# Differential attention on one core: both score maps of a step in one piece, the nine transposes in one piece behind them

## The chip, the cores and the metric

One core of a Trainium2 chip runs the whole program. The metric is the device time of one execution in microseconds (us); lower is better.

## The reference, cut to what matters

The program is one inference step of a two-layer backbone over 1024 latent and 128 context tokens: an even layer (long convolution and retention), an odd layer (differential attention), and after each a routed mixture of 16 experts. The change lies in the attention of the odd layer. Of each of 8 heads there are two maps of scores with 64 columns each; the second map's softmax, times lambda, is taken from the first's:

```python
def diff_attention(q, k, v, lam):
    B, Lq, H, _, d = q.shape
    nb = Lq // Q_BLOCK
    qb = q.reshape(B, nb, Q_BLOCK, H, 2, d).transpose(1, 0, 2, 3, 4, 5)
    scale = d ** -0.5

    def block(qi):
        s = jnp.einsum("bqhmd,bkhmd->bhmqk", qi, k).astype(jnp.float32) * scale
        p = jax.nn.softmax(s, axis=-1)
        a = p[:, :, 0] - lam * p[:, :, 1]
        return jnp.einsum("bhqk,bkhe->bqhe", a.astype(v.dtype), v)

    o = lax.map(block, qb)
    return o.transpose(1, 0, 2, 3, 4).reshape(B, Lq, H, 2 * d)
```

A block of 128 latent queries reads 1152 keys (1024 latent, 128 cached context); a block of context queries reads the 128 context keys alone. After the heads come a norm over each head's 128 columns and the output projection.

## The kernel before

All work is written out by hand, engine by engine, as straight lines of instructions with semaphores; nothing is rescheduled. The list `steps` has 72 steps (h, q): 8 heads, and for each 8 blocks of latent queries (q = 0 to 7) and one of context queries (q = 8). An iteration n of TensorE's loop (the function `attention`, from L1260) belongs to step n but computes the scores of step n + 2, so that softmax has time.

- `scores(n, m)` (L1219 to L1239) writes map m of step n into three of TensorE's result banks, 0 to 2 for m = 0 and 3 to 5 for m = 1. The contraction has 64 rows, so two multiplications stand beside each other in the two halves of the 128 rows: L1229 in one half, L1231 in the other (for this each head's queries and keys are also kept with halves swapped, in the ring buffer), then L1233 for the cached keys. The maps change halves. A context step has L1237 alone. Before it writes, it waits on `a.e` until ScalarE has read the same banks for step n - 1.
- On VectorE `maxima(n)` (L2108) takes the negated row maxima of both maps; on ScalarE `exps(n)` (L1560) turns both maps into exponentials in `eb` with their row sums; on VectorE `mix(n)` (L2116 to L2120) subtracts the scaled second map from the first.
- `turn` (L1241 to L1253) transposes the nine 128x128 pieces of the mixed map with TensorE. Eight (L1248) go to banks 6 and 7, four each; the ninth (L1253) goes to bank 6 again, so it waits on `a.tev` until ScalarE's first copy out of bank 6 is done. A context step has one piece.
- ScalarE's `evacuate` (L1568) copies bank 6, bank 7 and the ninth piece into `aT`.
- The product with the values (L1279, nine pieces added up in bank 7) waits on `a.tev` for the copies of bank 6 and bank 7; its ninth piece waits for the ninth copy. VectorE's L2135 reads the result and signals `a.oev`; L2137 sums its squares.
- At q = 2 of each head but the first, behind the product, the previous head's normed output is turned by the same nine transposes (called the head turn below) and copied by ScalarE to `yT`.

ScalarE's order in iteration n is `evacuate` of step n, then `exps(n + 2)`, then at q = 2 the copies of the head turn. VectorE's is `mix(n + 1)`, `maxima(n + 2)`, then L2135 of step n.

In the loop of TensorE the second map stands between the eight transposes and the ninth:

```python
                    if n + 2 < len(steps):
                        scores(n + 2, 0)
                    pe.wait_ge(*at("a.a", n + 1))
                    if n:
                        pe.wait_ge(*at("a.oev", n))
                    probs = lambda t: eb[:, n % 2, 0, t * P:(t + 1) * P]
                    turn(probs, done, nt, ninth=False)
                    if n + 2 < len(steps):
                        scores(n + 2, 1)
                    turn(probs, done, nt, first=False)
```

Of the kernel before, what the change touches and what calls it, by code (L numbers as in the profile page):

```python
# [109 lines left out]
def build(nc, a, out, tab):  # L110

    with ExitStack() as ctx:
# [32 lines left out]
        def common(name):  # L145
            head, _, tail = name.partition(".")
            pre, k = shared.get(head + ".", (head + ".", 0))
            name = pre + tail if _ else name
            base, off = carried.get(name, (name, 0))
            return base, off + (k * adds[base] if k else 0), name  # L150

        def s(name):

            name = common(name)[0]
            if name not in made:
                made[name] = ctx.enter_context(nc.semaphore(name))
            return made[name]
# [4 lines left out]
        def at(name, value):  # L162

            base, off, name = common(name)
            return s(base), value + off + ahead.get(name, 0)
# [230 lines left out]
        steps = [(h, q) for h in range(AH) for q in range(T)]  # L396
# [345 lines left out]
        def _(pe):  # L742
# [463 lines left out]
            def attention():  # L1206

                for h in range(AH):
                    i = tr(ps[:, 6 + h // 4, (h % 4) * P:(h % 4 + 1) * P], kTa[:, h, LAT:NT], ident[:, :])
                i.then_inc(s("a.kt"), 1)  # L1210
                pe.wait_ge(*at("a.ck", 16))
                for h in range(AH):
                    i = tr(ps[:, 4 + h // 4, (h % 4) * P:(h % 4 + 1) * P], ckrow[:, h * P:(h + 1) * P], ident[:, :])
                i.then_inc(s("a.kt"), 1)
                pe.wait_ge(*at("a.kctx", 2))
                pe.wait_ge(*at("a.ckT", 2))
                pe.wait_ge(*at("q.rope", 16))

                def scores(n, m):  # L1219

                    h, q = steps[n]
                    if n:
                        pe.wait_ge(*at("a.e", 2 * (n - 1) + m + 1))
                    if q < 8:
                        pe.wait_ge(*at(f"a.sw{h % 2}", 64 * (h // 2 + 1)))
                        near, far = slice(64 * m, 64 * m + 64), slice(64 - 64 * m, 128 - 64 * m)
                        own, other = qTa[near, h, q * P:(q + 1) * P], qTs[h % 2][far, q * P:(q + 1) * P]
                        for c in (0, 256):
                            mm(ps[:, 3 * m, c:c + 256], own, kTa[near, h, c:c + 256],  # L1229
                               start=True, stop=True, tile_position=(64 * m, 0))  # L1230
                            mm(ps[:, 3 * m + 1, c:c + 256], other, kTs[h % 2][far, c:c + 256],  # L1231
                               start=True, stop=True, tile_position=(64 - 64 * m, 0))
                        i = mm(ps[:, 3 * m + 2, 0:P], own, ckT[near, h, :],  # L1233
                               start=True, stop=True, tile_position=(64 * m, 0))
                    else:
                        near = slice(64 * m, 64 * m + 64)
                        i = mm(ps[:, 3 * m, 0:P], qTa[near, h, LAT:NT], kTa[near, h, LAT:NT],  # L1237
                               start=True, stop=True, tile_position=(64 * m, 0))
                    i.then_inc(s("a.s"), 1)  # L1239

                def turn(src, before, nt, first=True, ninth=True, oev=None):  # L1241

                    if first:
                        pe.wait_ge(*at("a.tev", before))
                        for t in range(min(nt, 8)):
                            if t == 4 and oev:
                                pe.wait_ge(*at("a.oev", oev))
                            i = tr(ps[:, 6 + t // 4, (t % 4) * P:(t % 4 + 1) * P], src(t), ident[:, :])  # L1248
                            if t % 4 == 3 or t == nt - 1:
                                i.then_inc(s("a.t"), 1)  # L1250
                    if ninth and nt == 9:
                        pe.wait_ge(*at("a.tev", before + 1))
                        tr(ps[:, 6, 0:P], src(8), ident[:, :]).then_inc(s("a.t"), 1)  # L1253

                for n in range(2):
                    for m in range(2):
                        scores(n, m)
                done = 0
                for n, (h, q) in enumerate(steps):
                    nt = 9 if q < 8 else 1  # L1260
                    if n + 2 < len(steps):
                        scores(n + 2, 0)
                    pe.wait_ge(*at("a.a", n + 1))
                    if n:
                        pe.wait_ge(*at("a.oev", n))
                    probs = lambda t: eb[:, n % 2, 0, t * P:(t + 1) * P]
                    turn(probs, done, nt, ninth=False)
                    if n + 2 < len(steps):
                        scores(n + 2, 1)
                    turn(probs, done, nt, first=False)  # L1270
                    done = tev_of[n]
                    pe.wait_ge(*at("a.tev", done - (nt == 9)))
                    if n == 0:
                        pe.wait_ge(*at("a.cv", 16))
                    for t in range(nt):
                        if t == 8:
                            pe.wait_ge(*at("a.tev", done))
                        v = cv[:, h * P:(h + 1) * P] if t == 8 else va[:, t if q < 8 else 8, h * P:(h + 1) * P]
                        i = mm(ps[:, 7, 0:P], aT[:, t * P:(t + 1) * P], v, start=t == 0, stop=t == nt - 1)  # L1279
                    i.then_inc(s("a.pv"), 1)  # L1280
                    if q == head_step and h:
                        pe.wait_ge(*at("a.on", h))
                        turn(lambda t: ohs[(h - 1) % 2][:, t, :], done, 9, oev=n + 1)
                        done = head_tev[h - 1]
                pe.wait_ge(*at("a.on", AH))
                pe.wait_ge(*at("a.oev", len(steps)))
                turn(lambda t: ohs[(AH - 1) % 2][:, t, :], done, 9)
                pe.wait_ge(*at("a.tev", head_tev[-1]))
                pe.sem_inc(s(f"slot{swap_unit % NS}_free"), 1)
# [11 lines left out]
            norm("n11.")  # L1301
            project("q.", odd_jobs)
            attention()
            out_project(1, outo_units)
            norm("n21.")
# [886 lines left out]
```

## Time and profile before

| | |
|---|---|
| time, median of 3 runs | 3970.93 us (3963.55 to 3975.09) |
| the profiled execution's own time | 3972.35 us |
| its span, first to last instruction | 3970.4 us |
| TensorE (PE) busy, mean granted clock | 3659.8 us (92%), 0.957 |
| VectorE (DVE) busy | 1724.4 us (43%) |
| ScalarE (ACT) busy | 800.1 us (20%) |
| GpSimd (POOL) busy | 412.3 us (10%) |
| DMA | 647.67 MB, 163 GB/s on average |

The shares are averages over stages with different limits. The span in 40 equal slices (busy tenths per slice, 99.3 us each):

```profile
PE   5987999888797999999989999999989799999996
DVE  5453002279625444444413220777733544444442
ACT  1013000112112111111121001656632111111112
PEclk8998999989897999999999999999999799999998
DMA  9661101212323788888880011000023388888886
```

The attention lies between 2470 and 2931 us, the 26th to the 30th digit: VectorE and ScalarE are busiest there, and DMA nearly rests. The two long stretches with DMA at 8 are the two expert mixtures.

### The profile page before, as it was taken

To read this page: it belongs to the slowest core of one execution; us is meant where nothing else is said; L and a number is where in the kernel's file an instruction comes from. 1 tells how busy PE (TensorE), PEld (TensorE's weight loads), DVE (VectorE), ACT (ScalarE), POOL (GpSimd) and SP (SyncE) were. 2 spreads that over 40 slices of the span, in tenths; PEclk is the share of its full clock that TensorE was granted. 3 is DMA by queue.
4 is the path that set the end of the run, shared out by engine and by line. 5 is a ranking of instruction groups with operands and counts; after the bars stand their busy time and mean duration, and the time that the engine had idled before them with its cause. 6 is when DMAs were issued, how large, how long until landed. Compare 5 with 4: busy or idle time off the path is not lost. (4 is left out here: it accounts for less than half of the span.)

```text
span 3970.4 us, 53619 instructions
## 1 busy us (share of the span) xinstructions
PE 3659.8 (92%) x22408; PEld 2883.8 (73%) x22408; DVE 1724.4 (43%) x4132; ACT 800.1 (20%) x1878; POOL 412.3 (10%) x547
## 2 busy tenths in 40 slices
PE   5987999888797999999989999999989799999996
PEld 2434545577546999999975554878854699999996
DVE  5453002279625444444413220777733544444442
ACT  1013000112112111111121001656632111111112
POOL 0111000009500000000000000111111000000001
PEclk8998999989897999999999999999999799999998
DMA  9661101212323788888880011000023388888886
GB/s 337 208 221 59 43 30 70 84 64 98 149 85 122 273 284 285 284 284 286 281 286 22 21 43 58 17 9 17 9 80 115 119 273 283 283 283 284 283 277 218
DMA packets 281331, 647.67 MB, mean 163 GB/s; under 512 B 9192, under 2 KB 9569, under 8 KB 279362
## 3 DMA queue, kind: packets, MB, share of 16 engines
q1 hardware_dynamic: 244626, 508.66, 35.6%
q0 software_dynamic: 36464, 135.58, 11.1%
q8 instruction: 178, 2.92, 0.3%
q14 instruction: 63, 0.52, 0.0%
HBM read 580.89 MB, written 57.02 MB: 161 GB/s over the span
## 5 line engine op out<-in xcount | busy, mean ns | idle before, releaser
L1153 PE MATMUL ps<-big,ring 128*128 128x144 f32 x8192 | 1031.7, 288 | 4.2 <-DVE big L2040 4.2
L1153 PEld LDWEIGHTS ps<-big,ring 128*128 128x128 f32 x8192 | 1014.6, 191 | 12.9 <-issue 11.6
L856 PE MATMUL ps<-hT,ring 128*128 128x384 f32 x1728 | 561.3, 489 | 5.8 <-issue 5.8
L1179 PE MATMUL ps<-big,ring 128*128 128x144 f32 x4096 | 512.0, 286 | 0.0
L1179 PEld LDWEIGHTS ps<-big,ring 128*128 128x128 f32 x4096 | 505.6, 190 | 0.0
L856 PEld LDWEIGHTS ps<-hT,ring 128*128 128x128 f32 x1728 | 330.3, 191 | 236.2 <-issue 10.1
L2068 DVE TENSOR_TENSOR big<-big,ps 128x144 f32<-128x144 f32 x256 | 77.9, 304 | 502.8 <-ACT big L1504 499.3
L1504 ACT ACTIVATE big<-ps 128x144 f32<-128x144 f32 x256 | 74.3, 290 | 979.8 <-PE ps L1153 979.8
L1034 PE MATMUL ps<-ring,yT 128*128 128x512 f32 x576 | 247.5, 592 | 0.0
L859 PE MATMUL ps<-ring,hT 128*128 128x512 f32 x576 | 247.5, 592 | 0.0
L2108 DVE TENSOR_REDUCE gst<-ps 128x1 f32<-128x1152 f32 x144 | 173.4, 1232 | 150.8 <-PE ps L1233 150.8
L2040 DVE TENSOR_SCALAR big<-ps,amul,modc 128x128 f32<-128x128 f32 x256 | 84.5, 402 | 319.4 <-PE ps L1106 319.2
L859 PEld LDWEIGHTS ps<-ring,hT 128*128 128x128 f32 x576 | 109.7, 190 | 137.1 <-issue 136.6
L1034 PEld LDWEIGHTS ps<-ring,yT 128*128 128x128 f32 x576 | 109.5, 190 | 136.6 <-issue 136.6
L1992 DVE TENSOR_SCALAR_CACHE_REDUCE yT<-big,yT 128x1024 f32<-128x1024 f32 (+1 forms) x240 | 193.9, 808 | 0.0
L1791 DVE TENSOR_SCALAR yT<-yT,colB 128x1152 f32<-128x1152 f32 x12 | 10.6, 880 | 379.9 <-ACT yT L1393 379.9
L1229 PE MATMUL ps<-big,yT 64*128 64x256 f32 x512 | 153.7, 424 | 23.6 <-ACT hT L1560 22.3
L1517 ACT ACTIVATE yT<-ps,modc 128x128 f32<-128x128 f32 x256 | 94.0, 367 | 394.9 <-PE ps L1179 394.9
L1560 ACT ACTIVATE hT<-ps,gst 128x1152 f32<-128x1152 f32 x144 | 160.9, 1122 | 29.9 <-DVE gst L2108 28.3
L1990 DVE TENSOR_SCALAR_CACHE_REDUCE yT<-big,yT 128x128 f32<-128x128 f32 (+6 forms) x210 | 156.1, 743 | 4.3
L1231 PE MATMUL ps<-ring 64*128 64x256 f32 x512 | 153.9, 424 | 0.0
L825 PE MATMUL ps<-big,hT 128*128 128x512 f32 x256 | 116.9, 613 | 19.1 <-DVE hT L1680 19.1
(367 smaller groups left out, 3987.9 us busy)
## 6 DMA issues: line engine op xcount, KB each, us to landing
ring<-in_moe_wg SPq DMA_DIRECT2D x64, 2048.0 KB, 10.2
ring<-in_moe_wu SPq DMA_DIRECT2D x64, 2048.0 KB, 13.4
ring<-in_moe_wd SPq DMA_DIRECT2D x64, 2048.0 KB, 11.4
ring<-in_w_mod SPq DMA_DIRECT2D x24, 2048.0 KB, 11.8
big<-aff_t POOLq DMA_DIRECT2D x30, 512.0 KB, 3.9
ring<-in_w_in_even SPq DMA_DIRECT2D x7, 2048.0 KB, 7.9
ring<-in_w_in_odd SPq DMA_DIRECT2D x6, 2048.0 KB, 10.1
big<-x_res POOLq DMA_DIRECT2D x24, 512.0 KB, 8.0
```

What stands on the lines that cost most here:

```text
L825: i = mm(ps[:, b + half, :], (fwd_c, fwd_s)[f][:, 4 * half + n, kt * P:(kt + 1) * P], FS[:, 4 * half + n, f, :], start=n == 0, stop=n == 3)
L856: i = mm(ps[:, b + g, 0:384], w[:, k, c * P:(c + 1) * P], hTv[:, k, g * 384:(g + 1) * 384], start=k == 0, stop=k == DK - 1)
L859: i = mm(ps[:, b, :], hTv[:, k, c * P:(c + 1) * P], w[:, k, :], start=k == 0, stop=k == DK - 1)
L1034: i = mm(ps[:, j % 4, :], yTv[:, k, t * P:(t + 1) * P], w[:, k, :], start=k == 0, stop=k == DK - 1)
L1153: last_mm = mm(ps[:, 3 + f % 2, g * CAP:(g + 1) * CAP], w[u - n0][:, k, c * P:(c + 1) * P], xsT[b][:, k, :], start=k == 0, stop=k == DK - 1)
L1179: last_mm = mm(ps[:, 3 + d % 2, 0:CAP], w[4 + d // 4][:, k, (d % 4) * P:(d % 4 + 1) * P], hid[:, k, :], start=k == 0, stop=k == DK - 1)
L1229: mm(ps[:, 3 * m, c:c + 256], own, kTa[near, h, c:c + 256], start=True, stop=True, tile_position=(64 * m, 0))
L1231: mm(ps[:, 3 * m + 1, c:c + 256], other, kTs[h % 2][far, c:c + 256], start=True, stop=True, tile_position=(64 - 64 * m, 0))
L1560: A(eb[:, n % 2, m, 0:w], bank(3 * m, 3)[:, 0:w], ACT.Exp, bias=gstf[:, c + 2 + m:c + 3 + m], accum_out=gstf[:, c + 4 + m:c + 5 + m]).then ...
L1990: ch.raised(ts(junk[:, 0:t0], row[:, 0:t0], mine, 0.0, ALU.is_ge, ALU.add, accum_out=cnt[:, t, 0:1]))
L1992: ch.raised(ts(junk[:, t0:LAT], row[:, t0:LAT], mine, 0.0, ALU.is_gt, ALU.add, accum_out=cnt[:, t, 1:2]))
L2108: nc.vector.tensor_reduce(gstf[:, c + 2 + m:c + 3 + m], bank(3 * m, 3)[:, 0:w], AX.X, ALU.max, negate=True).then_inc(s("a.nm"), 1)
```

## The change

Only TensorE's loop changes: `scores(n + 2, 1)` moves from behind the eight transposes to directly behind `scores(n + 2, 0)`. Nothing is added or removed; every wait stays with its own instruction.

```diff
@@ -1260,13 +1260,12 @@
                     nt = 9 if q < 8 else 1
                     if n + 2 < len(steps):
                         scores(n + 2, 0)
+                        scores(n + 2, 1)
                     pe.wait_ge(*at("a.a", n + 1))
                     if n:
                         pe.wait_ge(*at("a.oev", n))
                     probs = lambda t: eb[:, n % 2, 0, t * P:(t + 1) * P]
                     turn(probs, done, nt, ninth=False)
-                    if n + 2 < len(steps):
-                        scores(n + 2, 1)
                     turn(probs, done, nt, first=False)
                     done = tev_of[n]
                     pe.wait_ge(*at("a.tev", done - (nt == 9)))
```

On TensorE, in an iteration with nine pieces, before (the rows of the second map stand behind the eight transposes L1248; each L1229 or L1231 row is one multiplication with 256 columns, which the trace records as two instructions):

```order
L1229 MATMUL ps<-big,yT 128x256
L1231 MATMUL ps<-ring 128x256
L1229 MATMUL ps<-big,yT 128x256
L1231 MATMUL ps<-ring 128x256
L1233 MATMUL ps<-hT,yT 128x128
L1248 MATMUL ps<-ident_sb,hT 128x128 x8
L1229 MATMUL ps<-big,yT 128x256
L1231 MATMUL ps<-ring 128x256
L1229 MATMUL ps<-big,yT 128x256
L1231 MATMUL ps<-ring 128x256
L1233 MATMUL ps<-hT,yT 128x128
L1253 MATMUL ps<-ident_sb,hT 128x128
```

The product with the values, L1279, follows. In the same place of the changed kernel (one line number less from there on):

```order
L1229 MATMUL ps<-big,yT 128x256
L1231 MATMUL ps<-ring 128x256
L1229 MATMUL ps<-big,yT 128x256
L1231 MATMUL ps<-ring 128x256
L1233 MATMUL ps<-hT,yT 128x128
L1248 MATMUL ps<-ident_sb,hT 128x128 x8
L1253 MATMUL ps<-ident_sb,hT 128x128
L1278 MATMUL ps<-big,hT 128x128 x8
L1278 MATMUL ps<-hT 128x128
```

The five rows of the other map stand directly ahead of these, so that two groups of five follow each other and nothing is left between the eight transposes, the ninth and the product. The orders of ScalarE, VectorE, GpSimd and SyncE are unchanged but for the line numbers.

## Rows read from the trace of the kernel before

**Rows 1.** The profile page, chain that ended last, by line.

```profile
PE ps L1153 13%; PE ps L1179 6%; PE ps L1034 3%; PE ps L1184 0%; PE ps L1106 0%; ACT hT L1346 0%; DVE big L2169 0%; PE ps L1085 0%; DMA big<-x_res 0%; PE ps L1052 0%; DMA x_res<-big,yT 0%; DVE yT L1992 0%; PE ps L1022 0%; DVE yT L1990 0%; DMA big<-x_normed,yT 0%
```

**Rows 2.** Busy time by stretch, the whole attention and one head.

```profile
core 0: us, PE busy (x) PEld busy (x) DVE busy (x) ACT busy (x) POOL busy (x), PEclk, DMA share, GB/s
...
2656.50:2711.70 55.20, 51.79 (x394) 44.31 (x394) 43.05 (x74) 33.61 (x65) 8.71 (x23) 0.97 0.06 16
2470.00:2931.00 461.00, 420.75 (x3151) 359.98 (x3151) 342.30 (x592) 271.48 (x516) 66.51 (x173) 0.95 0.07 19
```

**Rows 3.** Timeline of TensorE, a plain iteration (head 3, q = 5).

```profile
start us, us, engine line op out<-in xcount [idle before <-releaser]
2682.20 0.48 PE L1229 MATMUL ps<-big,yT 64*128 64x256 f32 x1
...
2683.17 0.38 PE L1233 MATMUL ps<-hT,yT 64*128 64x128 f32 x2
2683.48 1.09 PE L1248 MATMUL ps<-ident_sb,hT 128*128 128x128 f32 x8
2684.50 0.48 PE L1229 MATMUL ps<-big,yT 64*128 64x256 f32 x1
...
2685.95 1.95 PE L1279 MATMUL ps<-big,hT 128*128 128x128 f32 x16
```

**Rows 4.** Timeline of ScalarE, the same iteration and the next.

```profile
2684.23 1.09 ACT L1568 ACTIVATE hT<-ps 128x512 f32<-128x512 f32 x2 [1.11 <-PE ps L1248]
...
2686.46 1.22 ACT L1560 ACTIVATE hT<-ps,gst 128x1152 f32<-128x1152 f32 x1
...
2687.67 1.21 ACT L1560 ACTIVATE hT<-ps,gst 128x1152 f32<-128x1152 f32 x1
...
2689.34 1.33 ACT L1568 ACTIVATE hT<-ps 128x512 f32<-128x512 f32 x3 [0.36 <-PE ps L1248]
```

**Rows 5.** Timeline of TensorE, the next iteration, q = 6 of head 3.

```profile
2688.05 0.48 PE L1237 MATMUL ps<-big,yT 64*128 64x128 f32 x2
2688.61 1.06 PE L1248 MATMUL ps<-ident_sb,hT 128*128 128x128 f32 x8
...
2690.02 0.33 PE L1253 MATMUL ps<-ident_sb,hT 128*128 128x128 f32 x1
2690.48 2.05 PE L1279 MATMUL ps<-big,hT 128*128 128x128 f32 x16
...
2692.68 0.48 PE L1229 MATMUL ps<-big,yT 64*128 64x256 f32 x1
```

**Rows 6.** Timeline of TensorE, attention's start, both maps of step 0 together.

```profile
2473.57 0.45 PE L1229 MATMUL ps<-big,yT 64*128 64x256 f32 x1 [1.33 <-issue]
...
2475.41 0.38 PE L1233 MATMUL ps<-hT,yT 64*128 64x128 f32 x2
```

**Rows 7.** Timeline of VectorE, the iteration of rows 3.

```profile
2683.22 0.17 DVE L2116 RECIPROCAL gst<-gst 128x2 f32<-128x2 f32 x1 [0.23 <-ACT hT L1560]
...
2685.02 2.62 DVE L2108 TENSOR_REDUCE gst<-ps 128x1 f32<-128x1152 f32 x2
```

**Rows 8.** Timeline of TensorE, from head 3 to head 4.

```profile
2701.35 0.49 PE L1279 MATMUL ps<-big,hT 128*128 128x128 f32 x2
2704.15 0.48 PE L1229 MATMUL ps<-big,yT 64*128 64x256 f32 x1 [2.32 <-ACT hT L1560]
...
2706.15 1.97 PE L1248 MATMUL ps<-ident_sb,hT 128*128 128x128 f32 x8
2708.05 0.48 PE L1229 MATMUL ps<-big,yT 64*128 64x256 f32 x1
...
2711.60 0.48 PE L1229 MATMUL ps<-big,yT 64*128 64x256 f32 x1
```

**Rows 9.** Timeline of TensorE, head 4, waits around its head turn.

```profile
2717.77 0.48 PE L1229 MATMUL ps<-big,yT 64*128 64x256 f32 x1 [0.26 <-ACT hT L1560]
...
2725.41 0.33 PE L1253 MATMUL ps<-ident_sb,misc 128*128 128x128 f32 x1 [0.62 <-ACT yT L1568]
```

**Rows 10.** Busy time and granted clock of two stretches (columns of rows 2).

```profile
2688.00:2692.70 4.70, 4.50 (x35) 3.69 (x33) 2.85 (x8) 3.11 (x9) 0.55 (x2) 1.00 0.57 147
...
2704.70:2708.00 3.30, 3.30 (x16) 2.58 (x12) 2.75 (x6) 1.20 (x3) 2.39 (x7) 0.50 0.00 0
```

## The prediction

> **What bounds the kernel now.** I read the chain that ended last first. Its lines are the experts' and the projections' [rows 1]; no line of the attention is among them, since everything behind the attention waits for its end and is then bound by TensorE itself. So a microsecond that the attention gains or loses is a microsecond of the kernel, and nothing outside it changes. Second, the busy times by stretch: the attention takes 461 us, and in one head TensorE is busy 51.79 of 55.20 us at a granted clock of 0.97 [rows 2]. Third, TensorE's timeline, where the reader should see one iteration as a sum without a gap [rows 3]: first map from 2682.20 to 2683.48, 1.28 us; eight transposes, 1.02; second map and ninth transpose from 2684.50 to 2685.95, 1.45; product with the values to 2688.05 [rows 5], 2.10. Together 5.85 us. TensorE is the bound of such an iteration. Fourth, ScalarE beside it: its copies out of banks 6 and 7 start at 2684.23, 0.75 us behind the first transpose, and both are done 1.09 later, 1.84 behind the first transpose [rows 4]. They lie wholly under the second map, so the product never waits for them.
>
> **What the change removes: two breaks per iteration.** A map alone takes 1.28 us. Two maps in a row stand once in this trace, at the attention's start: the first multiplication starts at 2473.57, the last group of the second map at 2475.41 [rows 6]; from such a last group to the next instruction it is 0.31 us (2683.17 to 2683.48, rows 3). So the pair takes 1.84 + 0.31 = 2.15 us, against 2 x 1.28 = 2.56: the last group of the first map, in one half of the rows, runs beside the first of the second map in the other half. Gain 0.41 us.
>
> **What it exposes: the copies.** With the second map gone from between, the ninth transpose has to wait for the copy of bank 6 and the product for that of bank 7. This pattern stands in the trace in the iterations at q = 6, eight of them, whose scores are of a context step and so short that they hide nothing: first transpose 2688.61, product 2690.48, 1.87 us behind it, then 2.20 to the next iteration at 2692.68 [rows 5], while the three copies run from 2689.34 to 2690.67 [rows 4]. Before, a plain iteration has 1.02 + 0.17 of transposes there; the rest, 0.68, becomes waiting. A plain iteration is then 2.15 + 1.87 + 2.20 = 6.22 us instead of 5.85: **0.37 longer**. Bounds: nothing of the 0.41 comes back, +0.78; or all of the wait stays hidden, -0.41. I take 0.37, since both its terms are rows of the same instructions.
>
> **Who waits for whom then.** The second map must wait on `a.e` for the exponentials of the second map one step earlier. ScalarE starts exponentials 2.1 us behind the first transpose when its three copies come in a row [rows 4, 5], 1.2 each, so both are read some 4.6 us behind it; TensorE comes back for the first map at 1.87 + 2.20 = 4.07 and for the second about 0.9 later (2.15 - 1.28), at 5.0. Some 0.4 us is left, so that wait is empty in plain iterations. VectorE's loop is the next bound: mix and both maxima take from 2683.22 to 2687.64 [rows 7]; the first maximum, which releases the exponentials, is done 3.1 us after the mix starts. Per iteration the exponentials' 2.4, these 3.1 and the hand-overs make some 5.8, about the old period; under 6.22 this loop has slack, but it is what is late next.
>
> **The other iterations of a head**, counted from one iteration's first score to the next's.
> - q = 6: 4.63 before (2688.05 to 2692.68), and its transposes start when L2135 has freed bank 7; the second context map took its time in the shade. 0, at most +0.2.
> - q = 7 and q = 8: 11.47 together (2692.68, rows 5, to 2704.15, rows 8), of which TensorE idles 2.32 at the end, waiting for an exponential. The chain through copies, exponentials, mix and maximum bounds this. The copies start 0.87 later but come in a row, so the exponentials start at the same moment; L2135 comes 0.37 later and pushes the mix by about 0.2. I take +0.2; bounds 0 and +0.4.
> - q = 0: behind that idle time the clock falls to 1.2 GHz, granted 0.50 from 2704.70 to 2708.00 [rows 10], and the eight transposes take 1.90 instead of 1.02 [rows 8]. At this level the pair of maps takes about 3.7 (the first map's 2.00, 2704.15 to 2706.15, and twice the 0.87 that a second map adds), ends where the slow stretch ends, and then the normal 4.07 follows, with 0.1 for its slow beginning: 7.90 against 7.45 (2704.15 to 2711.60). +0.45.
> - q = 1 and q = 2: they already hold waits for ScalarE, 0.26 for an exponential and 0.62 in the head turn, where transposes and ninth already stand as the change has them elsewhere [rows 9]. TensorE arriving later fills these first. 6.22 twice and a shorter head turn leave about -0.2 together; bounds -0.4 and +0.5.
> - q = 3, 4, 5: plain, 3 x 0.37 = 1.11.
>
> A head costs 0 + 0.2 + 0.45 - 0.2 + 1.11 = 1.56 us. Six such heads: 9.4. The last has no scores left behind q = 6: 1.36. The first has no head turn, so five plain iterations, 1.85, then 0.2 at its end, and for its start, where the same lower clock stands, I put 0.3, an estimate a little under the 0.45 of q = 0: 2.35. **Sum: +13.1 us.** Against the profiled execution's 3972.35 this gives 3985.4. That execution stands 1.4 above the median of the runs shown, 3970.93, so against the median I expect 3984. No DMA moves, no queue of SyncE or GpSimd is passed; GpSimd's reload of the swapped heads waits for score counts that come earlier, not later.
>
> **Rivals.**
> 1. *The order gains and the wait doesn't appear.* TensorE is full, two breaks go, and the product starts as early behind the transposes as now. It decides by the distance from the first transpose to the product: below 1.50 us (5.85 - 2.15 - 2.20) the change is faster; with no wait at all it gives -0.41 in the 26 plain iterations and some 10 beside them, -15 us, 3956. Against it stand the eight iterations at 1.87. The Trainium skill speaks for it: "TensorEngine Tiling (Array Packing)", under Tiling Modes, Key Properties, says that a change of tiling mode drains the array, and the old order has four such changes per iteration and the new one two. By that rule alone the time would be this rival's; the 0.41 of rows 3 and 6 agrees with it in sign. Chance 0.05.
> 2. *The slow stretches go.* Each head's 2.32 us of idle time shrinks to about 2.0, because the product at q = 8 itself now waits for a copy. If the clock then no longer falls, each of seven heads regains up to 0.72 on the first map (2.00 against 1.28) and 0.88 on the transposes, 1.6 us, 11 in all: about +2 us, 3973, no change. The stretch still holds almost no work, so I hold it unlikely: 0.10.
> 3. *The pair isn't one piece.* If the wait on `a.e` between the maps keeps them apart (a late exponential, or the wait itself), the 0.41 stays lost in some 36 iterations: +13 + 15 = +28, 3999. For it: VectorE's loop has little slack, and at the attention's start no such wait was open. Against: the 0.4 us of margin above. 0.13.
> 4. *The clock falls inside iterations.* Transposes, wait and ninth make 1.87 us in a row. Where the clock has fallen, transposes took 1.90 instead of 1.02; an iteration partly at 1.2 GHz would cost some 2 us more, in 64 iterations 128: about 4100. Against it: the iteration at q = 6 has the same stretch with still less work around it, and a granted clock of 1.00 throughout [rows 10]. "TensorE: Matmul & The Clock Gate", Part 4, in the Trainium skill says that transposes don't count as busy for the clock; by that rule the longer row of transposes and waiting speaks against the change, and the q = 6 rows show no fall. 0.05.
>
> **How the numbers follow.** My forecast, +13 with bounds of its own terms at +5 and +21, has 0.67. A measurement of this kernel can tell about 0.3%, 12 us, from no change, so the forecast lies on that border: a little over half of it, 0.39, is slower by more, 0.28 within. Rivals 3 and 4 add 0.18 to slower: 0.57. Rival 2 adds 0.10 to within: 0.38. Rival 1 is faster: 0.05. The range for 8 in 10 runs from just below rival 2's 3973, 3972, to a little above rival 3's 3999, 4002; outside lie rivals 1 and 4 and the edges of the rest.
>
> **What would show it.** In the new trace a plain iteration of 6.2 us with the last score group to first transpose as now, both maps within 2.15; a wait before the ninth transpose for ScalarE's L1568, and one before the product; the product 1.87 us behind the first transpose; q = 6 unchanged at 4.63; the clock still 0.5 once per head. The forecast is wrong if plain iterations stay at 5.85 or less, if waits on ScalarE's exponentials stand between the two maps, or if the granted clock falls within a head.

## The result and the profile after

The changed kernel takes 3987.98 us in the median of 5 runs (3986.8 to 3992.91), the kernel before 3970.69 (5 runs). The ratio is 1.0048, with a 95% interval from 1.0037 to 1.006: slower by a little more than the 0.3% that can be told from no change. The profiled execution takes 3986.8 us against 3972.35, 14.45 more, and its span 3984.9 against 3970.4. Of the runs below, one of the four executions of e4_other_bank (5563.16 us, granted clock 0.646) stands far from the other three and is left out of its figures.

All of it lies in the attention. From the first score to the first instruction of the output projection (L1022) it takes 474.10 us, 2471.30 to 2945.40; before it was 458.68, 2473.57 to 2932.25. That is +15.42; what precedes and follows differs by 1 us the other way.

TensorE's timeline of the changed kernel, the iterations q = 5 and q = 6 of head 3, answers to [rows 3, 5]:

```profile
2685.67 0.48 PE L1229 MATMUL ps<-big,yT 64*128 64x256 f32 x1
...
2687.82 1.09 PE L1248 MATMUL ps<-ident_sb,hT 128*128 128x128 f32 x8
2689.22 0.33 PE L1253 MATMUL ps<-ident_sb,hT 128*128 128x128 f32 x1 [0.31 <-ACT hT L1567]
2689.71 2.05 PE L1278 MATMUL ps<-big,hT 128*128 128x128 f32 x16 [0.15 <-ACT hT L1567]
...
2691.92 1.04 PE L1237 MATMUL ps<-big,yT 64*128 64x128 f32 x4
2692.89 1.09 PE L1248 MATMUL ps<-ident_sb,hT 128*128 128x128 f32 x8
...
2694.78 2.05 PE L1278 MATMUL ps<-big,hT 128*128 128x128 f32 x16 [0.16 <-ACT hT L1567]
...
2696.98 0.48 PE L1229 MATMUL ps<-big,yT 64*128 64x256 f32 x1
```

The reader should see three stretches. Both maps take 2685.67 to 2687.82, 2.15 us, as the attention's start [rows 6] had it. From the first transposition to the product it is 1.89, with two waits on ScalarE's copies that did not exist before; the product and its end take 2.21 instead of 2.10. The sum is 6.25 instead of 5.85. And q = 6 is 5.06 (2691.92 to 2696.98) instead of 4.63: from its first score to its first transposition it is now 0.97 instead of 0.56.

ScalarE beside it, which answers to [rows 4]:

```profile
2688.57 1.30 ACT L1567 ACTIVATE hT<-ps 128x512 f32<-128x512 f32 x3 [2.40 <-PE ps L1248]
2689.90 1.22 ACT L1559 ACTIVATE hT<-ps,gst 128x1152 f32<-128x1152 f32 x1
...
2692.22 0.20 ACT L1559 ACTIVATION_READ_ACCUMULATOR hT<-ps,gst 128x1 f32 x1
```

The three copies run in a row, 0.75 behind the first transposition; the exponentials start 2.08 behind it and are read to the end at 2692.42, 4.60 behind it. The second context map of q = 6 may only then be written, and the transpositions behind it start at 2692.89. PEld, TensorE's loading of weights, which stands ahead of each multiplication, shows the wait for it, 0.26 us:

```profile
2692.47 0.29 PEld L1237 LDWEIGHTS ps<-big,yT 64*128 64x128 f32 x2 [0.26 <-ACT hT L1559]
```

The waits of the attention, summed (engine and line, what it waited for: us in total, times, longest). Neither of the first two groups was long before; the third is q = 6's:

```profile
PE ps L1253 <- ACT hT L1567: 19.5, 62, 0.6
...
PE ps L1278 <- ACT hT L1567: 14.0, 72, 0.5
...
PEld ps L1237 <- ACT hT L1559: 2.1, 8, 0.3
```

VectorE reads each product (L2134, before L2135) as soon as it is there, so its starts are a clock for the iterations. Head 4 after the change (its first three products and its last two):

```profile
2716.64 0.35 DVE L2134 TENSOR_SCALAR hT<-ps,gst 128x128 f32<-128x128 f32 x1 [2.29 <-PE ps L1278]
2722.89 0.35 DVE L2134 TENSOR_SCALAR hT<-ps,gst 128x128 f32<-128x128 f32 x1 [0.80 <-PE ps L1278]
2729.13 0.35 DVE L2134 TENSOR_SCALAR hT<-ps,gst 128x128 f32<-128x128 f32 x1 [1.12 <-PE ps L1278]
...
2760.72 0.35 DVE L2134 TENSOR_SCALAR hT<-ps,gst 128x128 f32<-128x128 f32 x1 [2.19 <-PE ps L1278]
2765.77 0.34 DVE L2134 TENSOR_SCALAR hT<-ps,gst 128x128 f32<-128x128 f32 x1
```

From product to product, in us, the same head before and after (the head turn falls into the entry of q = 3):

| q | 0 | 1 | 2 | 3 | 4 | 5 | 6 | 7 | 8 | head |
|---|---|---|---|---|---|---|---|---|---|---|
| before | 7.83 | 5.84 | 6.18 | 7.90 | 5.85 | 5.85 | 4.63 | 5.85 | 5.23 | 55.16 |
| after | 8.26 | 6.25 | 6.24 | 7.80 | 6.24 | 6.25 | 5.06 | 6.24 | 5.05 | 57.39 |
| more | 0.43 | 0.41 | 0.06 | -0.10 | 0.39 | 0.40 | 0.43 | 0.39 | -0.18 | 2.23 |

Busy time by stretch of the changed kernel at the start of head 2, the start of head 4 and a plain iteration (stretch and its length, busy time of each engine, granted clock as the last number but two, DMA share, GB/s):

```profile
2593.90:2600.60 6.70, 6.07 (x47) 5.21 (x47) 5.25 (x10) 4.58 (x10) 4.31 (x17) 1.00 0.00 0
2709.40:2712.60 3.20, 3.20 (x19) 2.64 (x17) 2.69 (x5) 0.41 (x2) 2.46 (x8) 0.50 0.00 0
...
2685.70:2691.90 6.20, 5.73 (x48) 4.91 (x47) 4.99 (x8) 3.76 (x8) 2.12 (x4) 1.00 0.35 81
```

Nothing falls inside the plain iteration. At the start of a head the 1.2 GHz stretch stands as before (0.50 in head 4), but in heads 1 and 2 of this execution it didn't come at all (1.00). There the next iterations are longer instead. In head 2, behind the product of q = 0, VectorE's sum of squares (L2136) ran beside GpSimd's product of the previous head's norm (L716) and took 1.91 us. In plain iterations it takes 0.29, and in head 4, where it met only the end of L716, 0.61; both times it ended some 0.15 behind L716:

```profile
2600.79 2.11 POOL L716 TENSOR_TENSOR misc<-misc,gst 128x1152 f32<-128x1152 f32 x1
...
2601.14 1.91 DVE L2136 SCALAR_TENSOR_TENSOR misc<-hT 128x128 f32<-128x128 f32 x1
...
2607.69 0.48 PE L1229 MATMUL ps<-big,yT 64*128 64x256 f32 x1 [0.73 <-ACT hT L1559]
```

Mix, maxima and exponentials stand behind it on their engines' lists and came later, and TensorE's scores at q = 2 waited 0.73 us. Why VectorE is slower beside L716, no run was made to show.

### The profile page after: what moved, and what is told of

Read it like the earlier page. It is cut to its first block and busy times, and to the rows that moved or that the text cites. A ratio compares the mean times of both kernels' runs of the same rounds, so it can differ in the third digit from the quotient of the medians.

```text
span 3984.9 us, 53619 instructions
## 1 busy us (share of the span) xinstructions
PE 3652.5 (92%) x22408; PEld 2868.5 (72%) x22408; DVE 1722.6 (43%) x4132; ACT 796.7 (20%) x1878; POOL 412.3 (10%) x547
## 5 line engine op out<-in xcount | busy, mean ns | idle before, releaser
L1229 PE MATMUL ps<-big,yT 64*128 64x256 f32 x512 | 136.6, 406 | 21.8 <-ACT hT L1559 20.5
L1278 PE MATMUL ps<-big,hT 128*128 128x128 f32 x1040 | 135.2, 282 | 14.0 <-ACT hT L1567 14.0
L1231 PE MATMUL ps<-ring 64*128 64x256 f32 x512 | 145.1, 406 | 0.0
```

Source lines behind the costliest of these rows:

```text
L1229: mm(ps[:, 3 * m, c:c + 256], own, kTa[near, h, c:c + 256], start=True, stop=True, tile_position=(64 * m, 0))
```

## The experiments

The theory to be tested: the change wins 0.41 us per iteration by keeping the two maps together and loses 0.68 by baring ScalarE's copies and 0.10 in a product that starts behind a wait, plus what waits behind the second map at q = 6. Rivals: the pair itself does nothing; VectorE's chain is the bound; q = 6 is longer by its own rows.

**Break the pair (e1_break).** The changed kernel with one transposition between the maps:

```diff
                         scores(n + 2, 0)
+                        if steps[n + 2][1] < 8 and not (q == head_step + 1 and h):
+                            tr(ps[:, 6, 0:P], ident[:, :], ident[:, :])
                         scores(n + 2, 1)
```

> The changed kernel with one transposition of the identity into idle bank 6 between the two maps of a step (not in context steps, nor behind a head turn). Theory (a map on its own loses 0.41 us at its two ends, the pair saves that): the plain iteration goes from 6.25 to 6.25 + 0.41 + 0.13 for the transposition itself = 6.8 us; in some 45 iterations on TensorE's path +24 us, 4012. Rival (the pair saves nothing by standing together, and the 0.40 us come from a single wait): the transposition costs its own 0.13, plain iteration 6.4, +6 us, 3994.

4020.22 us, ratio 1.0128 (1.0113 to 1.0144) to the kernel before. TensorE's timeline of e1_break, a plain iteration (L1264 is the added transposition, L1280 the product):

```profile
2696.59 0.48 PE L1229 MATMUL ps<-big,yT 64*128 64x256 f32 x1
...
2697.86 0.33 PE L1264 MATMUL ps<-ident_sb 128*128 128x128 f32 x1
2698.12 0.48 PE L1229 MATMUL ps<-big,yT 64*128 64x256 f32 x1
...
2699.40 1.09 PE L1248 MATMUL ps<-ident_sb,hT 128*128 128x128 f32 x8
...
2701.29 2.05 PE L1280 MATMUL ps<-big,hT 128*128 128x128 f32 x16 [0.16 <-ACT hT L1569]
...
2703.50 0.48 PE L1229 MATMUL ps<-big,yT 64*128 64x256 f32 x1
```

The maps take 1.27 and 1.28 again, and the transposition 0.26 between its neighbours, twice its share in a row of eight (1.02 / 8). The plain iteration is 6.91, 0.66 more than 6.25: 0.41 for the broken pair and 0.26 for the piece between, against 0.41 + 0.13 expected. The copies' distance is unchanged, 1.89. So the pair's gain is real and of the predicted size. The whole came to 4020 instead of the 4012 expected; the piece's extra 0.13 us in 40 iterations is some 5 of these 8, and head 4, where the granted clock stood at 0.50 for 10 us, took 2.7 more than its neighbours. "TensorEngine Tiling (Array Packing)" in the Trainium skill says under Tiling Modes, Key Properties, that a change of tiling mode drains the array; it gives no price, and these rows are in line with it.

**Old order at q = 6 (e2_ctx_old, e2b_ctx_old).** Where the scores are a context step's, the second map stands behind the eight transpositions again:

```diff
+                    late = n + 2 < len(steps) and steps[n + 2][1] == 8
                     if n + 2 < len(steps):
                         scores(n + 2, 0)
-                        scores(n + 2, 1)
+                        if not late:
+                            scores(n + 2, 1)
...
                     turn(probs, done, nt, ninth=False)
+                    if late:
+                        scores(n + 2, 1)
```

> The changed kernel, but where the scores are of a context step (iterations q = 6) the second map stands behind the eight transposes again. Theory (the second context map waits for the exponential of the step before, and the transposes stand behind it): q = 6 falls from 5.06 back to 4.63 us, -3.4 us in all, 3984; plain iterations stay at 6.25. Rival (q = 6 is longer by its own rows on TensorE): it stays near 5.0.

The only execution of e2_ctx_old took 13233.84 us, with every stage of the program stretched, also those that the edit doesn't touch, so nothing is read from it. The same kernel ran again:

> The same kernel as e2_ctx_old once more: the changed order, but in iterations q = 6 the second (context) map stands behind the eight transposes again. Theory (the second context map waits for an exponential, and the transposes stand behind it): q = 6 falls from 5.06 back to 4.63 us, -3.4 us in all against the changed kernel, 3984. Rival (q = 6 is longer by its own rows on TensorE): it stays near 5.0.

3983.2 us, ratio 1.0037 (1.0024 to 1.0051). TensorE's timeline of e2b_ctx_old at q = 6:

```profile
2691.18 0.48 PE L1237 MATMUL ps<-big,yT 64*128 64x128 f32 x2
2691.74 1.06 PE L1248 MATMUL ps<-ident_sb,hT 128*128 128x128 f32 x8
...
2693.60 2.05 PE L1282 MATMUL ps<-big,hT 128*128 128x128 f32 x16
```

First score to first transposition is 0.56 again, first transposition to product 1.86, and the iteration 4.63 in all heads; plain ones stay at 6.25. So 0.43 in each of eight iterations, 3.4 us of the change's cost, is what the second context map costs ahead of the transpositions. That it is a wait this run doesn't show: the edit takes away the wait and also puts the map's own time back under the copies, so the rival would fall to 4.63 as well. The changed kernel's trace divides it: 0.26 is the wait (8 times, 2.1 us in all), some 0.15 the map's own time (0.97 - 0.26 - 0.56), and 0.02 the copies' distance. The time itself, 4.8 us lower in the median, is in line but alone would not show so small a step.

**Transpositions first (e3_turn_first).** The copies get the pair as their cover:

```diff
-                    if n + 2 < len(steps):
+                    probs = lambda t: eb[:, n % 2, 0, t * P:(t + 1) * P]
+                    own = q == head_step + 1 and h
+                    if own:
                         scores(n + 2, 0)
-                        scores(n + 2, 1)
                     pe.wait_ge(*at("a.a", n + 1))
-                    if n:
+                    turn(probs, done, nt, ninth=False, oev=n)
+                    if n and nt < 5:
                         pe.wait_ge(*at("a.oev", n))
-                    probs = lambda t: eb[:, n % 2, 0, t * P:(t + 1) * P]
-                    turn(probs, done, nt, ninth=False)
+                    if n + 2 < len(steps):
+                        if not own:
+                            scores(n + 2, 0)
+                        scores(n + 2, 1)
                     turn(probs, done, nt, first=False)
```

The wait on `a.oev`, for VectorE's reading of the product, moves too: it stands ahead of the fifth transposition, the first that writes bank 7, and no longer ahead of the first.

> The eight transposes stand ahead of both maps, the ninth behind them (behind a head turn the first map stays ahead). Theory (the change loses by the copies that nothing covers, and gains 0.41 by the pair): the copies lie under the pair, TensorE's own sum is 1.02 + 2.15 + 0.17 + 2.10 = 5.44 us, and the chain exponentials, mix, first maximum, exponentials of about 5.8 is the bound instead: plain iterations 5.7 to 5.9, 3960 to 3974, about the kernel before. Rival (the pair itself delays something, such as the exponentials that wait for it or the clock): plain iterations stay at 6.2, 3985 or more.

3964.69 us, ratio 0.9991 (0.9982 to 1.0). TensorE's timeline of e3_turn_first, q = 4 (L1282 is the product):

```profile
2724.95 1.27 PE L1248 MATMUL ps<-ident_sb,hT 128*128 128x128 f32 x8
2726.14 0.48 PE L1229 MATMUL ps<-big,yT 64*128 64x256 f32 x1
...
2728.29 0.33 PE L1253 MATMUL ps<-ident_sb,hT 128*128 128x128 f32 x1
2728.46 1.95 PE L1282 MATMUL ps<-big,hT 128*128 128x128 f32 x16
...
2730.47 1.26 PE L1248 MATMUL ps<-ident_sb,hT 128*128 128x128 f32 x8
```

The pair is 2.15, no wait stands before ninth transposition or product, and the iteration is 5.52. That is 0.73 less than in the changed kernel with the same instructions, about what the copies cost when nothing covers them. Three of a head's iterations (q = 4, 5 and 7) come to 5.52 to 5.57, less than the 5.7 to 5.9 expected; q = 0 to 3 stay at 5.85 or above, since VectorE's chain doesn't follow: in head 4 TensorE waits there for its reading of the product, 2.13 us at q = 0 and 0.97 at q = 2. Against the kernel before little is left: its interval touches 1.

**Product in bank 6 (e4_other_bank).** The changed order; the product starts behind the first copy, and the ninth transposition goes to bank 7 behind four of its nine pieces:

```diff
-                    turn(probs, done, nt, first=False)
-                    done = tev_of[n]
-                    pe.wait_ge(*at("a.tev", done - (nt == 9)))
+                    start, done = done, tev_of[n]
+                    pe.wait_ge(*at("a.tev", start + 1))
...
+                        if t == 4:
+                            turn(probs, start, nt, first=False, nb=7)
...
-                        i = mm(ps[:, 7, 0:P], aT[:, t * P:(t + 1) * P], v, start=t == 0, stop=t == nt - 1)
+                        i = mm(ps[:, 6, 0:P], aT[:, t * P:(t + 1) * P], v, start=t == 0, stop=t == nt - 1)
```

> The changed order, but the product is added up in bank 6 and needs only the first copy to start; the ninth transposition goes to bank 7 behind four of its multiplications. Theory (the distance from first transposition to product is the first two copies): it falls from 1.90 to about 1.4 us, and the plain iteration to 2.15 + 1.4 + 0.17 + 2.2 = 5.9 us; -14 us against the changed kernel, 3974. Rival (the product waits for something else, or VectorE's chain is the bound at 6.25): 6.2, 3986.

4027.5 us in the median of three executions, ratio 1.0145 (1.0127 to 1.0164): slower still, against the expectation. TensorE's timeline of e4_other_bank, a plain iteration (L1279 is the product here), and ScalarE's:

```profile
2699.49 1.09 PE L1248 MATMUL ps<-ident_sb,hT 128*128 128x128 f32 x8
2700.89 1.16 PE L1279 MATMUL ps<-big,hT 128*128 128x128 f32 x8 [0.31 <-ACT hT L1568]
...
2703.87 0.48 PE L1229 MATMUL ps<-big,yT 64*128 64x256 f32 x1 [0.59 <-ACT hT L1560]
```

```profile
2702.20 0.28 ACT L1568 ACTIVATE hT<-ps 128x128 f32<-128x128 f32 x1 [0.87 <-PE ps L1253]
2702.51 1.22 ACT L1560 ACTIVATE hT<-ps,gst 128x1152 f32<-128x1152 f32 x1
```

The part that the theory speaks of came out: first transposition to product is 1.40 instead of 1.89. What I had not looked at is the queue behind it. ScalarE copies the ninth piece before its exponentials, in program order, so these start 3.02 behind the first transposition instead of 2.08; TensorE's next scores then wait for them (0.59), and the plain iteration becomes 6.87.

**First maximum before the mix (e5_max_first, e5b_max_first).** The kernel before, with VectorE's order alone changed:

```diff
+                    if n + 2 < len(steps):
+                        maxima(n + 2, (0,))
                     if n + 1 < len(steps):
                         mix(n + 1)
                     if n + 2 < len(steps):
-                        maxima(n + 2)
+                        maxima(n + 2, (1,))
```

> The kernel before with another order on VectorE alone: first maximum of step n + 2, then the mix of step n + 1, then the second maximum. Theory (plain iterations are bound by TensorE, but the waits at the head's end, 2.3 us, and around q = 1 and 2 come from the chain exponentials, mix, first maximum, exponentials): plain iterations stay at 5.85, the wait at the head's end falls to about 1.2 us, 1 to 3 us per head are gained, 3945 to 3962. Rival (VectorE's chain is not what TensorE waits for there, or the mix comes too late then): 3968 or more, with new waits of the transposes for the mix.

> The kernel of e5_max_first once more, on the same chip as e8_mixed. Both theories: plain iterations 5.85, 3955 to 3965.

3961.94 us, ratio 0.9974 (0.9965 to 0.9983), and again 3961.18, 0.9977 (0.9967 to 0.9987): faster than the kernel before by less than 0.3%, but twice alike. Plain iterations stay at 5.85. TensorE's timeline of e5_max_first at a head's end:

```profile
2697.19 0.49 PE L1279 MATMUL ps<-big,hT 128*128 128x128 f32 x2
2698.64 0.48 PE L1229 MATMUL ps<-big,yT 64*128 64x256 f32 x1 [0.96 <-ACT hT L1560]
```

The wait there is 0.96 instead of 2.32 [rows 8], and heads take 53.1 to 54.8 us from product to product instead of 55.2 to 56.1. So that wait is VectorE's chain, as the prediction's term for q = 7 and 8 has it. Most of the time gained lies where the clock no longer fell: heads 1 to 3, which here have no stretch at 1.2 GHz, take 53.1, and heads 4 to 6, which have one (granted 0.50), 54.8. Head 4, with such a stretch in both kernels, falls only from 55.16 to 54.78.

**Both orders changed (e7_pair_max_first).** The changed kernel with e5_max_first's edit:

> The changed order on TensorE together with VectorE's other order (first maximum, mix, second maximum). Theory (the changed kernel's plain iteration is bound by TensorE and the copies, and the second map may start only when the second exponential of the step before is read): the copies keep costing their wait; the second maximum comes 1.9 us later, so the second exponential ends about 1.3 us into the next iteration where the second map wants to start at 0.9, the pair comes apart, 0.3 to 0.5 us more: plain iterations 6.5 to 6.8 instead of 6.25, q = 8 and 0 shorter by 1 to 3 us per head; 3980 to 3995 in all. Rival (VectorE's chain is what bounds the changed kernel): plain iterations fall below 6.25, under 3975.

4016.78 us, ratio 1.0108 (1.0089 to 1.0127), above what either theory gave. Plain iterations are 6.24 to 6.39: neither shorter, so VectorE's chain doesn't bound the changed kernel, nor as long as I expected. Most of the loss is at the start of each head: q = 0 takes 10.8 us instead of 7.0 to 8.6. Some 1.1 more stands at q = 6 (5.52 instead of 5.06) and q = 8 (5.67 instead of 5.04). Granted clock and TensorE's timeline of e7_pair_max_first there:

```profile
2726.00:2736.00 10.00, 9.03 (x39) 7.66 (x41) 4.64 (x8) 4.48 (x9) 6.53 (x18) 0.51 0.01 2
```

```profile
2723.67 0.48 PE L1229 MATMUL ps<-big,yT 64*128 64x256 f32 x1 [0.88 <-ACT hT L1559]
...
2726.66 0.79 PE L1229 MATMUL ps<-big,yT 64*128 64x256 f32 x1 [1.64 <-ACT hT L1559]
...
2731.74 3.78 PE L1278 MATMUL ps<-big,hT 128*128 128x128 f32 x16 [0.32 <-ACT hT L1567]
```

Here the pair does come apart: the second map waits 1.64 for an exponential. Behind the two waits the clock stands at 1.2 GHz for 10 us, and the product takes 3.78 instead of 2.05.

**A version from these parts (e8_mixed).** At q = 4 to 7 e3_turn_first's order on TensorE with VectorE's old order, elsewhere e5_max_first:

> In iterations q = 4 to 7 the order of e3_turn_first on TensorE (eight transposes, both maps, ninth) with VectorE's old order; in the others TensorE's order of the kernel before with VectorE's order of e5_max_first. Theory (copies covered by the pair let an iteration go down to 5.5 us where the chain through VectorE has slack, and the earlier first maximum gives that slack at the head's end): q = 4, 5 and 7 near 5.5, q = 8 to 3 as in e5_max_first, about 1 us per head better than it, 3950 to 3960. Rival (the chain is the bound everywhere, so the two gains don't add up): 3960 to 3968.

3953.19 us, ratio 0.9958 (0.9942 to 0.9974): faster than the kernel before and, with it, than the changed one; against e5b_max_first on the same chip 3953.19 to 3961.18, with intervals that overlap. TensorE's timeline of e8_mixed, q = 4:

```profile
2664.41 1.26 PE L1248 MATMUL ps<-ident_sb,hT 128*128 128x128 f32 x8
...
2669.93 0.60 PE L1248 MATMUL ps<-ident_sb,hT 128*128 128x128 f32 x4
2670.68 0.66 PE L1248 MATMUL ps<-ident_sb,hT 128*128 128x128 f32 x4 [0.15 <-DVE misc L2141]
```

5.52 us from transposition to transposition; the next one already waits 0.15 for VectorE. From product to product q = 7 takes 5.52, but q = 4 5.67 and q = 5 5.85, where the theory had all three near 5.5. Heads 1 to 5 take 52.7 us and head 6, with a stretch at 1.2 GHz, 54.4; in e5b_max_first heads take 53.1 without such a stretch and 54.8 with one. At like clock the order gains some 0.35 us per head, not the 1 us expected. Some 4 of the 8 us between the two kernels lie in heads 4 and 5, where the granted clock fell to 0.50 in e5b_max_first and stayed at 1.00 here.

## Why the prediction was right, and where it was short

- **The bound and the mechanism** stand. The chain of [rows 1] couldn't show that a microsecond of the attention is one of the kernel, since it reaches back only to 2929.11, 3 us before the attention ends; the result does (+15.42 in the attention, +14.5 in the span). The removed breaks gave 2 x 1.28 - 2.15 = 0.41, and e1_break, which puts them back, takes it again. The copies' distance came out at 1.89 against 1.87; e3_turn_first, which covers them, shows no wait, and e4_other_bank, which needs one copy less, 1.40. The plain iteration is 6.25 against 6.22.
- **q = 6 was mis-sized**: 0, at most 0.2, against 0.43 measured, of which 0.26 is a wait and some 0.15 the second context map's own time, no longer "in the shade" of the copies. The step "TensorE comes back for the second map about 0.9 later" holds for a latent map only. A context map is so short that TensorE comes back at once, and the exponential is done 0.5 us into the iteration. I had the numbers for it: 4.60 behind the first transposition against 4.07 and a little. In eight iterations the 0.43 make 3.4 us, and e2b_ctx_old returns them.
- **q = 1 to 3**: predicted -0.2 + 0.37 = 0.17 together, measured 0.41 + 0.06 - 0.10 = 0.37. The head turn shrank less than I thought.
- **q = 0, 7 and 8**: predicted 0.45 and 0.2, measured 0.43 and 0.21 in head 4. In the other heads q = 0 changed by -2.33 (head 1) to +0.75 (head 5), mostly by how long, and over which instructions, the clock stood at 1.2 GHz.
- Head 4 thus costs 2.23 instead of 1.56; 0.43 of the 0.67 between them is q = 6, 0.20 is q = 1 to 3. The attention costs 15.42 instead of 13.1 (in the medians the program costs 17.29).
- **That the sums lie so near is in part luck with the clock.** Heads 1 to 6 cost 12.08 (9.4 predicted), the last 1.99 (1.36), the first 1.35 (2.35). The first head's start was put at +0.3 and came out at -1.27: from the first score to VectorE's first reading of a product it takes 17.66 instead of 18.93. The kernel before stands at a granted clock of 0.50 twice there (2479.5 to 2482.7 and 2486.3 to 2489.5), the changed one once (2477.2 to 2480.4). And in heads 1 and 6 the kernel before stood at 0.50 for 6.5 us or more behind the same wait of 2.3 (2537.5 to 2544.0, 2814.0 to 2820.5), not for 3.3 as the prediction, which read one head, took for all; there q = 0 had 9.30 and 9.17 to lose.
- **Rival 1** (no wait appears) is refuted by the two waits. **Rival 2** came true in heads 1 and 2, without its price: q = 0 fell to 6.96, but q = 1 and 2 became 6.68 and 6.97, so that q = 0 to 2 make 20.61 against head 4's 20.75. TensorE, at full clock, came 1.3 us earlier, VectorE's L2136 then fell into GpSimd's L716 (1.91 us instead of 0.61), and the scores at q = 2 waited 0.73 for an exponential. The prediction had no term for that. **Rival 3**: the pair stays whole in plain iterations (2.15). It did come apart at q = 6, at q = 0 and 2 of heads 1 and 2 (2.48 and 2.49 instead of 2.15; the second map starts 0.05 behind the end of an exponential) and at the head starts of e7_pair_max_first, each time by the wait on `a.e`, as that rival has it. The prediction had named such a wait between the maps as a sign against itself; it stands outside the plain iterations alone. **Rival 4**: 1.00 in plain iterations. Their 1.89 us of transpositions and waiting brought no fall, so nothing here bears out as a cost the rule of "TensorE: Matmul & The Clock Gate", Part 4, in the Trainium skill, that transposes don't count as busy.

What stays open: why the clock at a head's start falls in some heads and not in others of one execution, and for 3.3 us in some and twice that in others; no run was made for it.

## What to carry to other kernels

An instruction group that stands between a producer and the consumer of its copy is a cover; before moving it, measure the distance from producer to consumer at a place where the cover is already missing, as q = 6 showed it here. Grouping like work saves its ends (0.41 us here), but only pays if the copies get other cover; with the transpositions first, the pair does both, where VectorE keeps up. And short special iterations need their own walk through the waits: what arrives in time behind long work arrives late behind short work.

## What the hardware showed that I had not expected

A single 128-row transposition between two groups of 64-row multiplications takes 0.26 us, twice its 0.13 in a row of eight, and the groups around it lose their overlap as well. And what follows a wait at a head's start differs at the same place of one program: behind the wait of 2.3 us the kernel before stood at 1.2 GHz for 3.3 us in five heads [rows 10] and for twice that in two, the changed one, behind 2.03, for 3.3 in five and not at all in two, and e5_max_first, behind 0.96, not at all in three. The two waits of 0.88 and 1.64 us of e7_pair_max_first, with one map between them, were followed by 10 us (0.51 granted) in every head but the first, which has no such waits.
